# mLSTM queries and keys turned by VectorE's 32x32 squares and a trip through memory instead of by TensorE

## The reference

```python
def _mlstm_mixer(x, w_in, conv_w, conv_b, gate_b, head_norm, w_out):
    proj = x @ w_in                       # 256 x 8208
    qk, v, o, gates, z = jnp.split(proj, [o1, o2, o3, o4], axis=-1)
    qk = jax.nn.silu(_causal_depthwise_conv(qk, conv_w, conv_b))   # 4 taps over time
    q, k = jnp.split(qk, 2, axis=-1)      # 8 heads of 128 each
    ...
    cell = _mlstm_chunkwise(q, k, v, i_pre, f_pre)
    cell = _rmsnorm(cell, head_norm)
    return (jax.nn.sigmoid(o) * cell * jax.nn.silu(z)) @ w_out
```

## Time and profile before

| | |
|---|---|
| median of 3 runs | 1828.15 us (1828.1 to 1828.44) |
| profiled execution: time, span of its trace | 1828.43 us, 1826.6 us |
| PE busy | 1813.7 us, 99% of the span |
| DVE, ACT busy | 69%, 52% |
| granted PE clock | 1.00, the 2.4 GHz level |

### The profile page before, as it was taken

The page is one execution under the profiler, slowest core; times in us unless marked ns, Lnnn a source line. Parts: engine busy times, 40 slices in busy tenths (PEclk is TensorE's granted clock), DMA queues, the critical chain, the costliest instruction groups (busy, mean ns, idle before and its releaser), DMA issues.

```text
span 1826.6 us, 24598 instructions
## 1 busy us (share of the span) xinstructions
PE 1813.7 (99%) x8999; PEld 1531.1 (84%) x8999; DVE 1267.3 (69%) x1711; ACT 942.7 (52%) x1310; POOL 38.0 (2%) x116
## 2 busy tenths in 40 slices
PE   8999999999999999999999999999999999999999
PEld 7899998888888888887888888888888888888887
DVE  6676766588556755767887878787767556577764
ACT  4545554455465555636554545555435444565542
POOL 2000000000000004000000000000000000000000
PEclk9999999999999999999999999999999999999999
DMA  8565454668889887575555555544547776555453
GB/s 293 162 177 148 139 175 156 202 179 185 177 153 212 175 179 176 191 238 159 174 175 152 167 173 154 179 154 160 185 138 232 217 217 209 162 160 163 159 166 113
DMA packets 172909, 323.61 MB, mean 177 GB/s; under 512 B 16584, under 2 KB 23136, under 8 KB 172048
## 3 DMA queue, kind: packets, MB, share of 16 engines
q1 hardware_dynamic: 171680, 317.89, 60.6%
q10 hardware_dynamic: 576, 4.19, 0.6%
q0 software_dynamic: 560, 0.26, 0.1%
HBM read 318.11 MB, written 4.19 MB: 176 GB/s over the span
## 4 chain that ended last, share of the span: by engine, by line
PE 98%; DVE 1%; ACT 0%; DMA 0%; issue 0%; DVEq 0%
PE acc L366 28%; PE acc L368 28%; PE acc L367 27%; PE ps L615 2%; PE ps L2760 2%; PE ps L463 1%; PE acc L332 1%; PE acc L333 1%; PE acc L331 1%; PE ps L648 1%; PE acc L350 0%; PE acc L349 0%; PE acc L353 0%; PE acc L355 0%; PE acc L348 0%; PE acc L354 0%
## 5 line engine op out<-in xcount | busy, mean ns | idle before, releaser
L299 DVE TENSOR_TENSOR wlo<-wraw,whi 128x1024 fp32r<-128x1024 f32 x579 | 699.1, 1222 | 337.4 <-ACT whi L284 334.4
L284 ACT ACTIVATE whi<-wraw 128x1024 fp32r<-128x1024 f32 x579 | 599.9, 1052 | 365.8 <-PE acc L368 333.4
L366 PE MATMUL acc<-whi,ta_hi 128*128 128x512 f32 x1664 | 659.7, 396 | 3.6 <-DVE ta_lo L548 2.0
L368 PE MATMUL acc<-whi,ta_lo 128*128 128x512 f32 x1664 | 649.2, 390 | 0.0
L367 PE MATMUL acc<-wlo,ta_hi 128*128 128x512 f32 x1664 | 647.8, 389 | 0.0
L366 PEld LDWEIGHTS acc<-whi,ta_hi 128*128 128x128 f32 x1664 | 312.6, 188 | 68.7 <-DVE ta_lo L548 3.4
L368 PEld LDWEIGHTS acc<-whi,ta_lo 128*128 128x128 f32 x1664 | 312.3, 188 | 66.9
L367 PEld LDWEIGHTS acc<-wlo,ta_hi 128*128 128x128 f32 x1664 | 312.8, 188 | 62.1
L366 PE MATMUL acc<-whi,tb_hi 128*128 128x512 f32 x576 | 228.4, 396 | 0.0
L368 PE MATMUL acc<-whi,tb_lo 128*128 128x512 f32 x576 | 224.9, 390 | 0.0
L367 PE MATMUL acc<-wlo,tb_hi 128*128 128x512 f32 x576 | 224.4, 390 | 0.0
(11 more groups left out here) (325 smaller groups left out, 1644.8 us busy)
## 6 DMA issues: line engine op xcount, KB each, us to landing
wraw<-in_ml_w_in SPq DMA_DIRECT2D x129, 512.0 KB, 5.8
wraw<-in_a_w_in SPq DMA_DIRECT2D x128, 512.0 KB, 3.9
wraw<-in_kv_w SPq DMA_DIRECT2D x64, 512.0 KB, 4.0
wraw<-in_b_w_in SPq DMA_DIRECT2D x64, 512.0 KB, 4.4
wraw<-in_mla_w_in SPq DMA_DIRECT2D x49, 512.0 KB, 4.6
wraw<-in_mla_w_out SPq DMA_DIRECT2D x32, 512.0 KB, 3.8
wraw<-in_ml_w_out SPq DMA_DIRECT2D x32, 512.0 KB, 4.4
wraw<-in_a_w_out SPq DMA_DIRECT2D x32, 512.0 KB, 3.8
```

Of the source, the lines that this page charges most:

```text
L284: nc.scalar.activation(unit_of(whi, n, SPLIT, w), unit_of(wraw, n, RAW, w), ACT.Copy).then_inc(w_high, 1)
L299: nc.vector.tensor_tensor(unit_of(wlo, n, SPLIT, w), unit_of(wraw, n, RAW, w), unit_of(whi, n, SPLIT, w).bitcast(F32), ALU.subtract).then_ ...
L366: nc.tensor.matmul(o, xh, wh, start=first, stop=False)
L368: m = nc.tensor.matmul(o, xl, wh, start=False, stop=end)
```

## The change

PE's eight transposes for each window go, and with them the semaphore `q_pe`. In their place:

- DVE turns 32x32 squares of the window (`qk_square`, two instructions of 128x512) into `cin`, right after it has brought its half of the tile out of PSUM.
- SP writes `cin` to `qk_squares` in memory behind the load of step at+8, where at is the step of that evacuation in `QK_EVAC`. Behind the load of step at+10 it waits for the write and reads the squares back into `qkw1` with four transfers (`turn_qk`).
- ACT's `window_in` waits for the four reads and copies from `qkw1` to `cin` in two instructions of 128x512, not from PSUM in one.
- `weigh` on PE takes over the wait for `tr_lo` that `window` had.

```diff
+        qk_squares = nc.dram_tensor("qk_squares", (P, 2 * COLS), F32).ap()
...
+        QK_EVAC = {(0, 0): 1, (0, 1): 10, (1, 0): 10, (1, 1): 18}
+        def qk_squares_of(v):
+            return cin[:, :, PAD:].rearrange("p j (b h c) -> p b j h c", b=TB, h=4)[:, v]
...
+            def turn_qk(name, p):
+                for (s, j), at in QK_EVAC.items():
+                    n = 2 * s + j
+                    if name == f"l1_{s}" and p == at + 8:
+                        sp.wait_ge(l1["q_sq"], TB * (n + 1))
+                        sp.dma_start(qk_squares.rearrange("p (j r) -> p j r", j=4), cin[:, :, PAD:]).then_inc(l1["q_out"], 16)
+                    if name == f"l1_{s}" and p == at + 10:
+                        sp.wait_ge(l1["q_out"], 16 * (n + 1))
+                        for i in range(4):
+                            rows = qkw1[32 * i:32 * i + 32, 1024 * j:1024 * j + 1024]
+                            sp.dma_start(rows.rearrange("q (i r) -> q i r", i=4),
+                                         qk_squares.rearrange("(i q) (j r) -> j q i r", i=4, j=4)[i]).then_inc(l1["q_in"], 16)
...
                     for p in range(units(tiles)):
                         load(name, p)
+                        turn_qk(name, p)
...
             def window_in(s, j):
                 n = 2 * s + j
-                act.wait_ge(l1["q_pe"], n + 1)
-                if n > 0:
-                    act.wait_ge(l1["y_ok"], 4 * n)
+                act.wait_ge(l1["q_in"], 64 * (n + 1))
                 act.wait_ge(l1["pads"], 2)
-                nc.scalar.activation(cin[:, :, PAD:], ps2(0).rearrange("p (h t) -> p h t", t=T),
-                                     ACT.Copy).then_inc(l1["q_c"], 1)
+                y = qkw1[:, 1024 * j:1024 * j + 1024].rearrange("p (i b h c) -> p b h i c", i=4, b=TB, h=4)
+                for b in range(TB):
+                    nc.scalar.activation(cin[:, :, PAD + b * P:PAD + (b + 1) * P].rearrange("p h (i c) -> p h i c", i=4),
+                                         y[:, b], ACT.Copy).then_inc(l1["q_c"], 1)
...
+            def qk_square(s, j):
+                landed(dve, *l1_at(s, j))
+                if 2 * s + j > 0:
+                    dve.wait_ge(l1["y_ok"], 4 * (2 * s + j))
+                for b in range(TB):
+                    v = qkw[j][:, b, :].rearrange("p (h j c) -> p j h c", h=4, j=4)
+                    nc.vector.transpose(qk_squares_of(b), v).then_inc(l1["q_sq"], 1)
...
-            def window(s, j):
-                landed(pe, *l1_at(s, j))
-                pe.wait_ge(tr_lo, turn.n)
-                if 2 * s + j > 0:
-                    pe.wait_ge(l1["q_c"], 2 * s + j)
-                if s > 0:
-                    pe.wait_ge(l1["st"], 4 * s)
-                for h in range(4):
-                    for b in range(TB):
-                        m = nc.tensor.transpose(ps2(0)[:, h * T + b * P:h * T + (b + 1) * P],
-                                                qkw[j][:, b, h * P:(h + 1) * P], ident[:])
-                m.then_inc(l1["q_pe"], 1)
...
             def weigh(s, c):
                 h = c % 4
                 pe.wait_ge(l1["q_r"], 2 * s + 2)
-                pe.wait_ge(l1["q_c"], 2 * s + 2)
+                if h == 0:
+                    pe.wait_ge(tr_lo, turn.n)
```

More of the change, by code:

```diff
@@ L794, in build @@
         L1_GATES = ("l1_g", 1)
-        l1 = sems(1, "g_in g_pe g_row g_e g_m g_pe2 g_col q_pe q_c y_ok y_e q_r sc arg ex sel st nm "
+        QK_EVAC = {(0, 0): 1, (0, 1): 10, (1, 0): 10, (1, 1): 18}
+        def qk_squares_of(v):
+            return cin[:, :, PAD:].rearrange("p j (b h c) -> p b j h c", b=TB, h=4)[:, v]
+        l1 = sems(1, "g_in g_pe g_row g_e g_m g_pe2 g_col q_sq q_out q_in q_c y_ok y_e q_r sc arg ex sel st nm "
                      "den h ssq var rs og ge z_ok pads")
@@ L2011, in gates_c @@
                 nc.vector.tensor_copy(acol, ps[:, 3, 0:16].rearrange("p (b h) -> p b h", b=TB)).then_inc(l1["g_col"], 1)
+            def qk_square(s, j):
[5 more added lines that the diff above has]
+                    nc.vector.transpose(qk_squares_of(b), v).then_inc(l1["q_sq"], 1)
             def conv(s, j, heads):
                 n = 2 * s + j
-                dve.wait_ge(l1["q_c"], n + 1)
+                dve.wait_ge(l1["q_c"], TB * (n + 1))
                 if s > 0:
@@ L2096, in l1_side @@
                 u = p if s else p + 8
+                for j in range(2):
+                    if p == QK_EVAC[(s, j)]:
+                        qk_square(s, j)
                 if s == 0 and p == 4:
@@ L2704, in l1_side @@
                     l1_rest(0, p)
-                for j in range(2):
-                    if u == L1_AT["qk"[j]]:
-                        window(s, j)
                 for h in range(4):
```

## The result

The changed kernel takes 1854.47 us (median of 4 runs, 1852.84 to 1856.71), the kernel before 1828.28 beside it (1828.10 to 1828.44). The ratio is 1.0144, interval 1.013 to 1.0157: 26.2 us slower. The profiled execution has a span of 1852.2 us, 25.6 above that of before (1826.6).

The account below looks back on a forecast made before the run. PE was taken to bound the kernel (busy 99%). Delays of DVE at (0, 1), (1, 0) and (1, 1), less its leads, made PE 18.6 us late: 1828.4 + 18.6 = 1847 us, range 1836 to 1853.

Parts of the forecast that it names:

- The removed work, 3.5 us: Four windows: PE loses eight transposes each, four times 0.87 us, 3.5 us in all, 0.19% of the kernel.
- SP's waits cost nothing: SP's queue: loads held 5 to 8 us behind its new wait cost nothing; without cover up to 3 us a window.
- The low price of 10.7 us: Write's issue to last read's landing takes 10.7 us, as read in layer four; used for windows (0, 0) and (1, 0).
- The sentence on the Trainium skill: Left out of the sum: the page's transfer fit puts the last read about 7.3 us after the write's issue, kernel near 1827.
- (0, 0) costs nothing: First window: reads in at 403.3, convolution starts at 404.6 and not 406.75; no delay, PE keeps its 0.87 us.
- (0, 1) and (1, 1) in order through the slow loads: Write and reads land in order among slow loads in SP's queue; convolutions start 6.0 and 10.3 us late.
- (1, 0) adds 3.4 us: Third window: loads are fast, data in at 596.9, convolution starts at 598.15 and not 594.75, 3.4 us late.
- The sum: DVE's delays over the windows, less its leads, make PE 18.6 us late: 1828.4 + 18.6 = 1847 us.
- Leads of 0.5 to 0.6 us: DVE is 0.5 to 0.6 us ahead of PE behind a convolution; one starting over 0.6 us later stops PE.
- The rival on the clock: PE's clock falls to half in two stops, 1.2 to 3 us each: 1849.5 to 1853 us; chance 0.22.
- The rival "equal and low": All windows have the 10.7 us turn-around, as squares pass between slow loads: PE +8.3, 1836.7 us; chance 0.22.
- The rival on the faster side: Data is back in time, all 3.5 us gained: 1824.9 or 1826 us; chance 0.04 faster by over 0.2%, 0.05 within.

Follow-up runs that it names:

- the first run: The changed kernel, but ACT copies the window unturned after DVE's transposes and nothing waits for the written and read data: 1824.82 us, ratio 0.998.

## Why the prediction was wrong, and what of it held

The direction and the way are as predicted. The size is not: 1854.47 us is 7.5 above the 1847 of the sum and 1.5 above the range's upper end, 1853.

**The removed work, 3.5 us.** Right, shown by the first run (PE busy 1810.2 against 1813.7, 1824.82 us in all).

**Transposes on DVE and copies on ACT hidden.** Right by the same run.

**SP's waits cost nothing.** Right by the same run, in which SP still waits for the write (up to 6.0 us, against 7.8 in the changed kernel) and the loads still stand behind it. In the changed kernel itself ACT never waited for a load in these stages.

**The low price of 10.7 us, used for (0, 0) and (1, 0).** This is the step that failed: the term of the turn-around in the two windows with fast loads was too small. Measured were 12.6 and 13.2 us. The 10.7 were read in layer four, where two loads stand between write and reads as well. What the price hides is when the second of them lands. The second load of layer four's first round, and that of window (0, 0) after the change:

```profile
L1016 SPq DMA_DIRECT2D wraw<-in_kv_w x1: 457/457/457, 1403.3 to 1403.3; - x1
...
DMA to landing us min/median/max: 6.4/6.4/6.4
...
L1023 SPq DMA_DIRECT2D wraw<-in_ml_w_in x1: 368/368/368, 397.1 to 397.1; - x1
...
DMA to landing us min/median/max: 6.7/6.7/6.7
```

Counted in us from the write's issue:

| | second load lands | last read lands (T) |
|---|---|---|
| layer four before, rounds 1 to 3 | 8.2 | 10.6 to 10.8 |
| layer four before, round 4 | 10.7 | 13.3 |
| (0, 0) | 10.4 | 12.6 |
| (0, 1) | 13.5 | 15.8 |
| (1, 0) | 9.9 | 13.2 |
| (1, 1) | 13.6 | 16.2 |

In every line the last read lands 2.3 to 3.3 us behind the second load. In window (0, 0) that load is issued 3.6 us behind the write and not 1.8, since it waits for a free buffer (the `low` that frees it ended at 397.05). In (1, 0) it is issued 2.2 behind, but takes 7.7 us to land and not 6.4; why is open. The prediction took 10.7 over whole, with the landing of 8.2 us in it, and passed over the fourth round, whose 13.3 us it had named and which was nearer to both windows. The loads are what T is made of: in the first window it is 7.8 us with nothing between, 9.4 with one load, 12.6 with two.

The sentence on the Trainium skill ("DMA: Bandwidth & Descriptors", "Anatomy of one DMA") had an estimate of 7.3 us for T. The page gives its fit for transfers that GpSimd issues; these are SP's. The 7.3 are close to the 7.8 of the runs with nothing between, but the time near 1827 was reached only with places moved as well: with T at 7.7 to 8.5 us and the places as they were it was 1829.84. For the kernel as changed the estimate was 5 to 9 us short, since the fit has no term for the loads ahead.

**(0, 0) costs nothing.** True of PE (no stop there), but the convolution began at 407.27 and not at 404.6. 1.9 of these 2.7 us are T; the other 0.8 is the write, issued at 393.44 and not at 392.6, since two more instructions of DVE (L1828, L1833) lie between the evacuation and the transposes. By that the keys of (0, 1) left PSUM later than I had it. The row on DVE and the write of (0, 1) on SP:

```profile
420.69 0.68 DVE L412 COPY arena<-acc 128x512 f32<-128x512 f32 x1
421.47 1.31 DVE L2042 STREAM_TRANSPOSE arena<-arena 128x512 f32<-128x512 f32 x2
...
422.80 0.55 SPq L1051 DMA_DIRECT2D qk_squares<-arena  x1
```

W is 422.80, not 420.05: 2.75 us of the difference at (0, 1), where the convolution was to be 6.1 late and was 9.2.

**(0, 1) and (1, 1) in order through the slow loads.** Right. From W to the reads I had 15.5 and 16.4 us, and T was 15.8 and 16.2, with the second load landing 13.5 and 13.6 behind W (I had 13.05 and 13.9). The delay that (1, 1) added was forecast as 10.3 us and came out as 10.3 (25.6 less 15.3).

**(1, 0) adds 3.4 us.** It added 6.1, by the low price again.

**The sum.** DVE's own delays were forecast as 6.0, 3.4 and 10.3, together 19.7, and measured as 9.2, 6.1 and 10.3, together 25.6. 5.9 of the 7.5 us that I was short are these two terms. Another 1.1 are the leads of 0.5 and 0.6 that the sum took off for PE: by the spans PE ended 25.6 us late, as late as DVE. The last 0.5 lies between the median and the profiled execution (1853.99 us). What ate the leads is not shown; the half clock is a candidate, but with the clock kept at 1.00 the profiled span was the same.

**Leads of 0.5 to 0.6 us.** Right in kind: PE's waits for `wlo` came behind each window that was late by more, and at none other, the largest at the keys.

**The rival on the clock.** Its mechanism was right and came three times, not twice, also behind a stop of 4.5 us. Its price of 1.2 to 3 us for each stop looks too high: the medians differ by 1.9 us for three stops and the profiled spans by nothing, since most of the slow work lay in time that PE would have spent waiting. That the time came out nearer to this rival's 1853 than to 1847 is luck: the low price put it there, not the clock.

**The rival "equal and low".** Wrong: T differs by about 3 us between the windows with fast loads and those with slow ones. The rival on the faster side asked for T under 9.4, 7.4 and 6.1 us. The run with write and reads a step earlier had 8.5, 8.0 and 7.7: it met the first bound and missed the others by 0.6 and 1.6 us. DVE lost 0.6 and 1.8 us there, so these bounds held.

What stays open: why the last of four reads lands about 2 us behind the third in the fast windows (median 5.1, maximum 7.1 us in (0, 0)).

## What to carry to other kernels

In these runs a round trip through memory that replaces engine work costs itself plus the loads that are still on their way when its reads are issued. So price it with them, and put the reads straight behind the write, before any load. A T read elsewhere in the same program may be taken over only with the loads that stood in it and the time at which they landed, and where the rounds differ (10.7 and 13.3 here) the slow one needs a reason before it is left out. When an engine waits for such a trip, look at the lead of each engine that follows it (here 0.5 us), and remember that a delay early in a stage moves the issue of the next trip as well.

## What the runs showed of the hardware that was not expected

- Loads of the same size from the same matrix are of two kinds by the column block that they read. `ml_w_in` has rows of 8208 floats. With even blocks of 512 columns alone, the median landing fell from 6.2 to 4.4 us, and the DMA engines moved 198 GB/s at a busy share of 0.76, where an odd block took 0.98 for 167. Why is open; only that the block decides is shown.
- A second queue gave no way past the loads of the first (T 12.5 against 12.6 us in the first window, 18.8 against 15.8 in the second), and four reads took ACT 4.68 us to issue in the second window, against 3.19 on SP.
- The granted clock fell to half in a stop of 4.5 us as well as in those of 8.2 and 8.5. What the three spells cost together is not clear of the spread (1.9 us between the medians, nothing between the profiled spans).
